# Another order for the first weights and activation tiles of a gated encoder layer, and weight by weight turns in its second stage

## The reference, cut to what matters

```python
h = rmsnorm(x, g_pre)
xa, ba, ca, za, xb, zb, ga, gb = split(h @ w_in)       # 8 sections of 1024 columns
u  = ca * xa
ya = ((ba * (conv_b + conv3(u))) * silu(za)) @ w_a_out
d  = trailing_mean(xb, W_g) - xb                        # W = 2, 4, 8, 16 by channel group
yb = ((d @ w_grp) * pool_scale * silu(zb)) @ w_b_out
m  = sigmoid(ga) * ya + sigmoid(gb) * yb
x1 = x + rmsnorm(m @ w_o, g_post)
out = x1 + (p @ w_ple) * sigmoid(x1 @ w_pgate)
```

## Time and profile before

| | us |
|---|---|
| median of 3 runs (759.38 to 759.58) | 759.58 |
| the profiled execution's own time | 759.77 |
| its span, slowest core (8 cores: 756.5 to 758.2) | 758.2 |
| PE busy | 745.3 (98%) |
| DVE busy | 384.3 (51%) |
| POOL busy | 339.8 (45%) |
| ACT busy | 254.3 (34%) |

### The profile page before, as it was taken

One profiled execution on the slowest core, in us unless ns is written; L12 is line 12 of the kernel. 1 busy time (PEld: TensorE's weight loads), 2 busy tenths in 40 slices (PEclk: granted clock), 3 DMA queues, 4 the chain that ended last, 5 costly groups with the idle time before them and its releaser, 6 DMA issues.

```text
span 758.2 us, 13217 instructions; the slowest of 8 cores (756.5 to 758.2 us)
## 1 busy us (share of the span) xinstructions
PE 745.3 (98%) x4386; PEld 376.5 (50%) x4386; DVE 384.3 (51%) x639; ACT 254.3 (34%) x514; POOL 339.8 (45%) x514
## 2 busy tenths in 40 slices
PE   6899999999999999999999999999999999999998
PEld 5665454444444444454545545455455555555444
DVE  4775667776622112455557666575751212224655
ACT  3533444442211111333333333343421111115453
POOL 5333555558642433342435536466582342211544
PEclk9999999999999999999999999999999999999999
DMA  8999769858995564827547384474747354306643
GB/s 184 219 149 195 92 156 167 155 109 130 172 156 78 75 92 61 139 76 138 87 85 129 78 135 79 90 132 63 152 84 119 56 80 63 55 0 202 157 119 125
DMA packets 65907, 87.82 MB, mean 116 GB/s; under 512 B 30897, under 2 KB 34737, under 8 KB 65842
## 3 DMA queue, kind: packets, MB, share of 16 engines
q0 software_dynamic: 29792, 50.41, 45.1%
q1 hardware_dynamic: 36050, 36.57, 17.4%
HBM read 117.35 MB, written 11.36 MB: 170 GB/s over the span
## 4 chain that ended last, share of the span: by engine, by line
PE 93%; DMA 4%; POOL 1%; DVE 1%; issue 1%; ACT 0%; SPq 0%; DVEq 0%; ACTq 0%; POOLq 0%
PE ps L604 74%; PE ps L829 8%; PE ps L876 7%; DMA w<-w_in 2%; PE ps L882 2%; DMA wo<-x 2%; PE ps L745 1%; PE ps L575 0%; PE ps L781 0%; POOL sp L713 0%; POOL mT L595 0%; DVE hb L562 0%; DVE sg L894 0%; ACT hb L555 0%; DVE qT L897 0%
## 5 line engine op out<-in xcount | busy, mean ns | idle before, releaser
L604 PE MATMUL ps<-hB,w 128*128 128x512 bf16 (+1 forms) x912 | 156.5, 326 | 0.0
L604 PE MATMUL ps<-hA,w 128*128 128x512 bf16 (+1 forms) x816 | 143.6, 329 | 2.6 <-DVE hA L579 1.9
L604 PEld LDWEIGHTS ps<-hB,w 128*128 128x128 bf16 x912 | 77.1, 98 | 72.0
L604 PE MATMUL ps<-hB,hA 128*128 128x512 bf16 (+1 forms) x624 | 108.6, 326 | 0.0
L604 PEld LDWEIGHTS ps<-hA,w 128*128 128x128 bf16 x816 | 69.2, 98 | 69.0 <-issue 3.7
L808 DVE SCALAR_TENSOR_TENSOR tA<-tA,ps 128x512 f32<-128x512 f32 (+1 forms) x40 | 24.3, 609 | 141.5 <-PE ps L604 141.5
L604 PE MATMUL ps<-hA,mT 128*128 128x512 bf16 x400 | 91.4, 379 | 0.0
L811 POOL TENSOR_TENSOR mT<-tA,tB 128x512 bf16<-128x512 f32 (+1 forms) x40 | 44.0, 1109 | 84.4 <-DVE tB L808 84.0
L604 PEld LDWEIGHTS ps<-hB,hA 128*128 128x128 bf16 x624 | 52.8, 98 | 49.1
L805 ACT ACTIVATE tA<-ps 128x512 f32<-128x512 f32 (+1 forms) x40 | 21.3, 533 | 152.3 <-PE ps L604 147.5
L876 PE MATMUL ps<-wpg,x1T 128*128 128x512 bf16 (+2 forms) x296 | 61.7, 362 | 0.0
(11 more groups left out here) (131 smaller groups left out, 903.0 us busy)
## 6 DMA issues: line engine op xcount, KB each, us to landing
w<-w_in POOLq DMA_DIRECT2D x75, 256.0 KB, 7.3
hA<-w_in POOLq DMA_DIRECT2D x26, 256.0 KB, 8.0
hA<-x SPq DMA_DIRECT2D x10, 512.0 KB, 3.5
y<-hA SPq DMA_DIRECT2D x10, 512.0 KB, 3.8
mT<-w_in POOLq DMA_DIRECT2D x19, 256.0 KB, 8.7
wo<-x SPq DMA_DIRECT2D x9, 512.0 KB, 8.2
wpg<-x SPq DMA_DIRECT2D x8, 512.0 KB, 13.9
w<-w_b_out POOLq DMA_DIRECT2D x14, 256.0 KB, 5.5
```

The lines of the kernel that those rows point to most:

```text
L604: ins_ = e.matmul(bk.ap[:, parts[0]:parts[1]], lhsT=w.ap[:, kk, :], rhs=act(kk), start=(kk == 0), stop=(kk == 7))
```

## The change

1. **First loads.** x tiles 0 to 4 come first (SP issues them in a row). The weights of j = 0 are issued when tile 1 has landed. Tiles 5 to 7 wait until the sixth weight has landed, and the w_xbt blocks until tile 5 has landed.
2. **Who copies.** The transposed tiles of half 1 go from PSUM to `hA` on ACT and no longer on DVE. The multiplication into `hb` is one instruction of 1024 columns, except for tile 0.
3. **Products.** The first block (tiles 0 to 3) runs tile by tile only for j = 0. The second block is cut for j = 0 and 1 into tile 4 alone and tiles 5 to 7; for j = 0 the latter goes in two pieces, tile 5 and then tiles 6 and 7 as one.
4. **Fold.** The two slots of a folded weight are taken when w_grp is loaded, and no longer when PE has folded.
5. **Gain.** The row of ones is one partition, the zeroing of 128 partitions (L468, L469) is gone, and the load of g_pre waits for nothing.
6. **Stage 2.** The key of a group now rises weight by weight, not block by block. The loads of w_o and w_pgate for j > 1 also wait for the first block's gate products of the j before.
7. **Planner.** `DMA_RATE` is a table over time; the keys of 'pow' and of the fold's copies are lower.

```diff
-DMA_RATE = 0.30
+DMA_RATE = ((0.0, 0.36), (4.4, 0.20), (7.0, 0.33), (46.0, 0.30))
...
-        OP('dve', lambda e, d: d(e.memset(vT_[:].bitcast(F32)[:, 0:1024], 0.0)), 0.6, -60.0, outs=[res("vT_reg")], tag='grow0')
-        OP('dve', lambda e, d: d(e.memset(ones[:], 0.0)), 0.2, -47.0, outs=[res("ones")], tag='ones')
-        OP('dve', lambda e, d: d(e.memset(ones[0:1, :], 1.0)), 0.1, -46.9, ins=[res("ones")], outs=[res("ones")], tag='ones1')
+        OP('dve', lambda e, d: d(e.memset(ones[0:1, :], 1.0)), 0.1, -47.0, outs=[res("ones")], tag='ones')
...
-            for h in range(2):
-                o = OP('dve', lambda e, d, h=h: d(e.scalar_tensor_tensor(
-                    out=hb.ap[:, h * 512:(h + 1) * 512], in0=x.ap[:, h * 512:(h + 1) * 512], scalar=stats[:, gi, 2:3],
+            cols = ((0, 512), (512, 1024)) if gi == 0 else ((0, 1024),)
+            for c0, c1 in cols:
+                o = OP('dve', lambda e, d, c0=c0, c1=c1: d(e.scalar_tensor_tensor(
+                    out=hb.ap[:, c0:c1], in0=x.ap[:, c0:c1], scalar=stats[:, gi, 2:3],
...
+                if ev == 'act':
+                    OP('act', lambda e, d: d(e.copy(out=hv[:, :, tl.rel:tl.rel + 128], in_=tb.ap[:].bitcast(BF16).rearrange("p (k c) -> p k c", k=8))),
+                       0.9, key + 0.6, ins=[tb], outs=[hreg(tl)], tag=f'ev{gi}')
...
-            g8 = 8 * mm_us(N)
+            g8 = 8 * mm_us(N) + sum(8 * mm_us(kb.N) for kb in others)
+            key = key + sum(8 * mm_us(kb.N) * (1 if others else 4) for kb in halves[k.half].blocks[:k.b])
...
-        for n, tl in enumerate(H1.tiles[:4]):
-            norm(tl, -20.0 + n, -38.0 + n + (1.0 if n else -1.5), True, loaded=(x0, x0_load) if n == 0 else None)
+        for n, tl in enumerate(H1.tiles[:5]):
+            norm(tl, -20.0 + n, -38.0 + n + (1.0 if n else -1.5), True, loaded=(x0, x0_load) if n == 0 else None, ev='act', hbs=[p_hb, p_hq] if n > 2 else None)
...
-        load_secs(0, 0, -32.0, [p_w, p_wm], (0, 1, 2, 3))
-        load_secs(0, 1, -22.0, [p_w, p_wm], (0, 1, 2, 3), [H1.tiles[0].pow])
-        for n, tl in enumerate(H1.tiles[4:]):
-            norm(tl, -10.0 + n, -32.0 + n, True, hbs=[p_hq])
-        wt = load_wt(0, -14.0, [p_w, p_wm])
+        load_secs(0, 0, -32.0, [p_w, p_wm], (0, 1, 2, 3), [H1.tiles[1].load])
+        load_secs(0, 1, -22.0, [p_w, p_wm], (0, 1, 2, 3))
+        for n, tl in enumerate(H1.tiles[5:]):
+            norm(tl, -10.0 + n, -32.0 + n, True, hbs=[p_hq, p_hb], load_after=[w_ops[(0, 1, 1)]], ev='act')
+        wt, wf = load_wt(0, -14.0, [p_w, p_wm], [H1.tiles[5].load])
...
+        p1_conv(0, b0, wins[(0, 1, 0)], kp, (0, 1, 2, 3))
+        p1_conv(1, b0, wins[(0, 1, 1)], kp + 4 * G8, None)
         for j in range(2):
-            for k in H1.blocks:
-                p1_conv(j, k, wins[(0, 1, j)], kp + (2 * j + k.b) * 4 * G8 + (6.0 if k.b else 0.0), j == 0)
+            p1_conv(j, parts[0], wins[(0, 1, j)], kp + 8 * G8 + j * G8, None)
+        for j in range(2):
+            p1_conv(j, parts[1], wins[(0, 1, j)], kp + 10 * G8 + 3 * j * G8, (0, 1) if j == 0 else None)
...
-                   outs=[res(f"{name}{kk}")], dma=0.524, sem=f"ld_{name}{kk}", after=norm_done, tag=f'{name}{kk}')
+                   outs=[res(f"{name}{kk}")], dma=0.524, sem=f"ld_{name}{kk}", after=norm_done + (p2_done[-1:] if j > 1 else []), tag=f'{name}{kk}')
```

More of the change, by code:

```diff
@@ L28, with dma_rate @@
 MM = 0.2157
+def dma_rate(t):
+    return [r for t0, r in DMA_RATE if t0 <= t + 1e-9][-1]
 def mm_us(n):
@@ L222, in ring_step @@
                     return
-                rate = DMA_RATE / len(heads)
-                end = min([dma_t + r[0][1] / rate for r in heads] + nxt + [t])
+                rate = dma_rate(dma_t) / len(heads)
+                end = min([dma_t + r[0][1] / rate for r in heads] + nxt + [t] + [t0 for t0, _ in DMA_RATE if t0 > dma_t + 1e-9])
                 for r in heads:
@@ L238, in ring_next @@
             if heads:
-                rate = DMA_RATE / len(heads)
-                return min([dma_t + r[0][1] / rate for r in heads] + nxt)
+                rate = dma_rate(dma_t) / len(heads)
+                return min([dma_t + r[0][1] / rate for r in heads] + nxt + [t0 for t0, _ in DMA_RATE if t0 > dma_t + 1e-9])
             return min(nxt) if nxt else None
@@ L542, in build_program, with norm @@
         early_tr = []
-        def norm(tl, key, key_load, pe_tr, load_after=(), hbs=None, hold=0.0, loaded=None):
+        def norm(tl, key, key_load, pe_tr, load_after=(), hbs=None, hold=0.0, loaded=None, ev='dve'):
             gi = tl.gi
@@ L547, in norm @@
             hb = Buf(hbs or [p_hb], f"hb{gi}")
+            pk = -60.0 + gi if gi < 8 else key + 0.3
             if loaded is not None:
@@ L631, in p1_groups @@
             if tilewise:
-                for n, tl in enumerate(k.tiles):
+                for n in tilewise:
+                    end = min([c for c in tilewise if c > n] + [len(k.tiles)])
                     for i, g in enumerate(gs):
-                        c0 = n * 128
-                        go = group(key + 1.73 * max(i, n) + 0.1 * n + 0.01 * i, bks[i], 128, (c0, c0 + 128), ws[g],
-                                   lambda kk, tl=tl: hv[:, kk, tl.rel:tl.rel + 128], [ws[g], hreg(tl)], n == 0, f'p1t_{j}_{k.b}_{g}_{n}')
+                        c0, c1 = n * 128, end * 128
+                        go = group(key + 1.73 * max(i, n) + 0.1 * n + 0.01 * i, bks[i], c1 - c0, (c0, c1), ws[g],
+                                   lambda kk, c0=c0, c1=c1: hv[:, kk, k.rel + c0:k.rel + c1], [ws[g]] + [hreg(t) for t in k.tiles[n:end]], n == 0, f'p1t_{j}_{k.rel // 128}_{g}_{n}')
                         gops.append(go)
@@ L790, in p2_unit @@
             N = k.N
+            others = [kb for kb in halves[k.half].blocks if kb is not k] if (k.half, j) != (1, 7) else []
             hv = hT[k.half]
-            g8 = 8 * mm_us(N)
+            g8 = 8 * mm_us(N) + sum(8 * mm_us(kb.N) for kb in others)
+            key = key + sum(8 * mm_us(kb.N) * (1 if others else 4) for kb in halves[k.half].blocks[:k.b])
             bks = [bank() for _ in range(4)]
@@ L975, in build_program @@
         kp = T_P1[0]
+        b0 = H1.blocks[0]
+        parts = []
+        for lo, hi in ((4, 5), (5, 8)):
+            k = Blk()
+            k.half, k.b, k.samp, k.N, k.rel, k.tiles = 0, 1, False, (hi - lo) * 128, lo * 128, H1.tiles[lo:hi]
+            parts.append(k)
+        p1_conv(0, b0, wins[(0, 1, 0)], kp, (0, 1, 2, 3))
+        p1_conv(1, b0, wins[(0, 1, 1)], kp + 4 * G8, None)
         for j in range(2):
-            for k in H1.blocks:
-                p1_conv(j, k, wins[(0, 1, j)], kp + (2 * j + k.b) * 4 * G8 + (6.0 if k.b else 0.0), j == 0)
+            p1_conv(j, parts[0], wins[(0, 1, j)], kp + 8 * G8 + j * G8, None)
+        for j in range(2):
+            p1_conv(j, parts[1], wins[(0, 1, j)], kp + 10 * G8 + 3 * j * G8, (0, 1) if j == 0 else None)
         kp += 16 * G8
-        wf = fold(0, wt, kp, [p_w, p_wm])
+        fold(0, wt, wf, kp)
         for j in range(2):
@@ L987, in build_program @@
             pools = [p_w, p_wm] if jp < 3 else [p_wm, p_w]
-            wt = load_wt(jp, (kp - 42.0) if jp > 1 else -8.0, pools)
+            wt, wf = load_wt(jp, (kp - 42.0) if jp > 1 else -8.0, pools)
             for j in (2 * jp, 2 * jp + 1):
@@ L1008, in build_program @@
         norm_done = list(norm_ops)
+        p2_done = []
         rl = []
@@ L1028, in build_program @@
             for k in H1.blocks:
-                p2_unit(j, k, wins[(0, 2, j)], kj + k.b * 4 * 8 * MM, all_p1 if j == 0 else ())
+                p2_unit(j, k, wins[(0, 2, j)], kj, all_p1 if j == 0 else ())
+            p2_done.append(H1.blocks[0].p2h[-1])
         gateA = [o for k in H1.blocks for o in k.p2h]
```

43 lines of the change are left out of this document (21 added, 22 removed).

## The result

The kernel before takes 759.58 us (median of four runs, 759.38 to 760.29), the changed kernel 763.90 us (median of five, 763.08 to 766.58). Their ratio is **1.0058, 95% interval 1.0040 to 1.0075**: slower by 4.3 us, where 756.0 was forecast.

A forecast was written before the change was run, and what follows sets the result against it. PE was taken as the bound, busy 745.3 of 758.2 us. 759.77 - 3.4 (start) + 0.5 (tiles 5 to 7) - 0.7 (stage 2) = 756.2, median 0.2 lower: 756.0 us; own range 754.6 to 757.4, 8 in 10 753.4 to 758.5.

The forecast's parts named there:

- The end of the program is untouched: 0.: Program's end: the change was taken to alter nothing there, 0 us.
- From there 8 groups and 512 column groups stand ready, so it runs on.: Stage 1, from tile 4's transpose at 21.1 us: PE has work ready and does not stop again.
- Landings: Start: tile 1 lands at 8.1 us, tiles 2 and 3 at 9.7 and 11.4, the first weight at 13.8.
- The chain of tiles 0 to 4: Start, norm and transposes up to tile 4: a gain of 3.4 us, two cases of 2.9 and 3.8 weighted equally.
- case B: Start: the gain's load lands near 5.5 us, tile 4's transpose starts at 20.2; gain 3.8 us, weighted one half.
- Tiles 5 to 7, 0.5 (0 to 3): Start, later x tiles: landing by about 32 us, they lose 0.5 us, bounds 0 and 3.
- Stage 2, 0.7: Stage 2: PE's wait for a weight goes, a gain of 0.7 us, bounds 0 and 0.7.
- the half clock: Rival, start: PE falls to 1.2 GHz between 13 and 21 us, making the kernel slower, 762 us; chance 0.06.
- The new order gives most of it back: Rival, start: stage 1 waits for later-issued weights and tiles 5 to 7, 2.4 us lost again, 758.4 us; chance 0.19.
- ScalarE and PSUM: Copies to `hA`: skill puts ScalarE closer to PSUM; ACT's copy at DVE's 0.69 us would make the gain 0.7 larger.

The follow-up runs named there:

- the spread alone: The kernel before, with only the later loads of w_o and w_pgate (j > 1, waiting for the first block's gate products of the j before) added: 1.0058.
- e3: Changed kernel with w_o and w_pgate issued as early as before, weight by weight keys kept: only two times, 759.41 and 762.1 us, beside 761.16 of the kernel before.
- c4: c5 with each warm-up group as two products of 256 columns instead of four of 128: 0.9993 of the kernel before.
- c5: Changed kernel, w_o and w_pgate early; tile 5 released by fifth weight, 6 and 7 by sixth, w_xbt and wgrp by eighth, later weights by tile 7's 'pow': 1.0004.
- c6: c4 with DVE's convolution step moved behind tile 5's gain product and the last tile copied out by DVE instead of ACT: 0.9988 of the kernel before.
- h1: Changed kernel with each group of four 128-column warm-up products at the start made one product of 512 columns: 1.0047 of the kernel before.
- c1 to c3: Changed kernel, w_o and w_pgate early, tile 5 and w_xbt gates moved: 1.0030; plus 512-column warm-ups: 1.0043; plus late w_o and w_pgate, early POOL drain: 1.0044.

## Why the prediction was wrong, step by step

- **"The end of the program is untouched: 0."** This step failed, and it decides the sign. The spread lengthened POOL's closing drain from 4.97 to 10.29 us; measured, the end is 3.3 us later on the slowest core. The diff does not touch the end, and I looked no further. The drain stood in the trace of before, 1.5 us short of the last store, as a cover that could go; I had not read it, since no view of waits shows an instruction that computes nothing. Shown by adding the spread alone (1.0058), taking it away (a drain of 4.98 us) and draining early (1.0000).
- **"From there 8 groups and 512 column groups stand ready, so it runs on."** The second failure, worth 1.3 us on the median core and 2.6 at most. The operands stood ready; the instructions did not. The description of the kernel before says that on the chip only semaphores hold an instruction back; the pauses behind records 443 and 699 are instructions that no semaphore holds. (The 1.3 us count the one core without the pause as 0.)
- *Landings.* Tile 1 squared at 7.91 (8.1 forecast), tiles 2 and 3 at 9.80 and 11.25 (9.7 and 11.4). The first weight came not at 13.8 but 15.8, 2.0 late, and PE waited for it for 0.44 us; all of that was covered again by the norm chain.
- *The chain of tiles 0 to 4.* Right, in case B: the gain products begin at 5.70, the multiplication of 1024 columns takes 1.28 us (1.3), ACT's copy 1.01 (1.06), tile 4 is transposed at 20.26 (20.2). By then the loss is 20.3 - 5.4 = 14.9 us, a gain of 3.7 of the 3.8 forecast for this case. It was given back behind 22 us.
- *Tiles 5 to 7, 0.5 (0 to 3).* On the profiled core 0.6; on three others the wait ahead of tile 5 was 0.7, 0.8 and 2.2, on the remaining four at most 0.2. The 2.2 us stand on core 4, the one without the nameless pause. A mis-sized term for the slowest of eight: what counts there is the worst landing, and the time of a program is that of its slowest core.
- *Stage 2, 0.7.* Right: that wait is gone, the window from 200 to 300 us is busy for 100.00. Before, it was on three cores of eight (0.9, 0.7 and 0.2 us). Turns alone (e3, c4, c5) and the spread alone each leave it on none, so one of the two was superfluous, and it was the spread that cost 3.3 us elsewhere.
- *The rivals.* The slower case came, but not by the half clock: stage 1's products run at 0.056 us (24 in 1.50 us from 18.75 on), as before. The prediction's argument against it, the granted clock of 1.00 in the earlier trace rows, was no argument: the warm-ups from 9.38 on run at the lower level, 24 in 2.74 us, up to about 13.8, in a window whose granted clock is 1.00 as well. Only the time of a product tells the level. From the forecast to 761.1 it is also 5.1 us, not 5.4. "The new order gives most of it back" was right for the start, by another mechanism: its condition, 2.5 us more for the first weight, was almost met and cost 0.4.
- *ScalarE and PSUM.* ACT's copy took 1.01 us against DVE's 0.69, as the row had it, and not as the prediction drew it from the Trainium skill ("VectorE: DVE Perf Modes", Specifications); c6 has the last copy back on DVE.

What stays open: the rule by which the spread, or a dozen small transfers, changes the drain. That it is POOL's transfers, how many and where they stand, and that an earlier drain takes over most of it, is shown; whether their order or their times matter is not, since a gate moves both; a count of transfers, a period of 32 and unbounded growth are excluded. The runs also don't say why PE's instruction packet comes when it does, nor why c4's last stores take longer.

## What to carry to other kernels

Read what every engine does after its last useful instruction, and compare it with the last store: a closing drain of an engine that issues many transfers can be the end of the program, is seen only on its own line, and moves with the order of transfers hundreds of us earlier. If it is too long, drain once where that engine is idle. When TensorE stops with "issue", count its records: at a constant count it is its instruction stream that is late, and fewer or wider instructions ahead of that place let PE arrive there later in time. And in a start bound by transfers a pause that is removed can come back at the next landing, as in h1 and c1 to c3: look at the last chain (landing, square, 'pow', product), not only at the first. Last, when a change has two halves that aim at the same wait, run each alone: here one was enough, and the other cost all of the loss.

## What the runs showed of the hardware that I had not expected

- POOL's closing drain takes 1.8 to 10.6 us, the same within some 10 ns on each of eight cores, and goes with POOL's transfers: 20 more memsets 0.0 us, 10 more small transfers +5.06, 12, 22 and 32 more on top of the changed kernel +0.33, -2.04 and -2.86.
- A drain in mid-program took 4.2 to 14.3 us.
- TensorE stood still for up to 2.7 us at fixed counts of its stream, 256 records apart, and went on 0.9 to 1.6 us after the end of a 16 KB packet of the instruction queue. 102 or 68 warm-up records fewer moved or removed the pause.
- The granted clock of a window was 1.00 while 24 products in it took 2.74 us, which is the lower of the two levels (1.2 GHz).
